# A projection in rounded parts: twelve more units per layer, contraction pieces outside, four units side by side in PSUM

## The reference

```
h = rms_norm(x, mix_norm[l])
p = h @ w_in[l]                # 1024 x 3200; in layer 1 also h @ vres_w_in (16 columns)
p_rwkv, p_conv, p_attn = p[..., :1280], p[..., 1280:2048], p[..., 2048:]
x = x + concat([rwkv7(p_rwkv), short_conv(p_conv), dilated_attention(p_attn)]) @ w_o[l]
x = x + ffn(rms_norm(x))       # layer 0: dense SwiGLU; layer 1: top 2 of 8 experts
```

## Time and profile before

| | us |
|---|---|
| median of three timed runs | 1656.16 |
| profiled execution, all of it | 1657.62 |
| its span | 1655.8 |
| TensorE busy in the span | 1605.9 |
| VectorE busy | 1213.1 |
| ScalarE busy | 1032.0 |
| projection of layer 0, first product to chunk 1's first | 21.05 to 93.05 |
| projection of layer 1, the same | 472.77 to 552.64 |

### The profile page before, as it was taken

The page is one execution under the profiler, slowest core; times in us unless marked ns, Lnnn a source line. Parts: engine busy times, 40 slices in busy tenths (PEclk is TensorE's granted clock), DMA queues, the critical chain, the costliest instruction groups (busy, mean ns, idle before and its releaser), DMA issues.

```text
span 1655.8 us, 28409 instructions
## 1 busy us (share of the span) xinstructions
PE 1605.9 (97%) x10904; PEld 1388.1 (84%) x10904; DVE 1213.1 (73%) x1378; ACT 1032.0 (62%) x1282; POOL 61.5 (4%) x70
## 2 busy tenths in 40 slices
PE   7998999999999999999999999999999999999997
PEld 6887889999988878888888888888888888888885
DVE  1465454545424664699999999999999999999996
ACT  2334344444423343488888888888887887888885
POOL 0003000000000040000000000000000100000000
PEclk8999999999989999899999999999999999999999
DMA  6502165555414301799999999999999999999994
GB/s 215 185 1 105 53 230 187 188 184 179 160 57 149 107 3 65 268 374 375 348 393 392 345 395 394 353 395 385 357 393 381 362 394 362 377 395 358 386 385 142
DMA packets 192503, 446.11 MB, mean 269 GB/s; under 512 B 9104, under 2 KB 11680, under 8 KB 192288
## 3 DMA queue, kind: packets, MB, share of 16 engines
q1 hardware_dynamic: 187040, 433.49, 71.4%
q0 software_dynamic: 2160, 7.87, 2.0%
q10 hardware_dynamic: 3216, 3.53, 0.6%
HBM read 438.56 MB, written 6.29 MB: 269 GB/s over the span
## 4 chain that ended last, share of the span: by engine, by line
PE 95%; DVE 2%; issue 1%; ACT 1%; DMA 0%; POOL 0%; SPq 0%; DVEq 0%; ACTq 0%; POOLq 0%
PE bank L700 24%; PE bank L702 24%; PE bank L701 24%; PE bank L683 15%; PE bank L796 3%; PE bank L1248 1%; PE bank L708 1%; DMA arena<-in_consts 0%; PE bank L1045 0%; ACT acts_hi L1312 0%; DVE acts_lo L2110 0%; PE bank L803 0%; DVE w_lo L1853 0%; DVE ring L1708 0%; PE bank L692 0%
## 5 line engine op out<-in xcount | busy, mean ns | idle before, releaser
L1312 ACT ACTIVATE w_hi<-ring 128x1024 fp32r<-128x1024 f32 x772 | 815.5, 1061 | 292.7 <-PE bank L702 292.0
L1862 DVE TENSOR_TENSOR w_lo<-ring,w_hi 128x1024 fp32r<-128x1024 f32 x672 | 812.9, 1224 | 64.1 <-ACT w_hi L1312 16.5
L700 PE MATMUL bank<-w_hi,acts_hi 128*128 128x512 f32 x1344 | 528.3, 393 | 7.1 <-DVE acts_lo L2110 5.7
L702 PE MATMUL bank<-w_hi,acts_lo 128*128 128x512 f32 x1344 | 523.7, 390 | 0.0
L701 PE MATMUL bank<-w_lo,acts_hi 128*128 128x512 f32 x1344 | 523.5, 389 | 0.0
L700 PEld LDWEIGHTS bank<-w_hi,acts_hi 128*128 128x128 f32 x1344 | 252.4, 188 | 59.8 <-issue 5.9
L702 PEld LDWEIGHTS bank<-w_hi,acts_lo 128*128 128x128 f32 x1344 | 252.3, 188 | 52.9
L701 PEld LDWEIGHTS bank<-w_lo,acts_hi 128*128 128x128 f32 x1344 | 252.5, 188 | 50.9
L1853 DVE TENSOR_TENSOR w_lo<-ring,w_hi 128x1024 fp32r<-128x1024 f32 x84 | 102.7, 1225 | 118.4 <-ACT w_hi L1312 118.4
L700 PE MATMUL bank<-acts_hi,w_hi 128*128 128x256 f32 x608 | 174.2, 286 | 1.6 <-DVE acts_lo L1671 1.6
L701 PE MATMUL bank<-acts_lo,w_hi 128*128 128x256 f32 x608 | 173.1, 285 | 0.0
(11 more groups left out here) (210 smaller groups left out, 1216.5 us busy)
## 6 DMA issues: line engine op xcount, KB each, us to landing
ring<-in_moe_wg SPq DMA_DIRECT2D x112, 1024.0 KB, 6.9
ring<-in_moe_wu SPq DMA_DIRECT2D x112, 1024.0 KB, 7.2
ring<-in_moe_wd SPq DMA_DIRECT2D x112, 1024.0 KB, 6.9
ring<-in_w_in SPq DMA_DIRECT2D x24, 1024.0 KB, 6.7
ring<-in_dense_wg SPq DMA_DIRECT2D x14, 1024.0 KB, 5.1
ring<-in_dense_wu SPq DMA_DIRECT2D x14, 1024.0 KB, 5.1
ring<-in_dense_wd SPq DMA_DIRECT2D x14, 1024.0 KB, 4.8
ring<-in_w_o SPq DMA_DIRECT2D x8, 1024.0 KB, 7.4
```

The source lines that it names most:

```text
L700: pe.matmul(out_, a_hi, b_hi, start=first, stop=False, **kw)
L702: return pe.matmul(out_, a_lo, b_hi, start=False, stop=final, **kw)
L1312: return act.activation(o, i, ACT.Copy, **kw)
L1862: TT(w_lo[:, q, :], raw, w_hi[:, q, :].bitcast(F32), ALU.subtract).then_inc(lo_ready, 1)
```

## The change

`SPLIT_IN` becomes (4, 5, 2, 0, 1): chunks 4, 5 and 0 are split too. Chunks 4, 5, 2 and 0 run through a new function, `project_together`: the four pieces of the contraction are the outer loop, and inside it the chunk's units take turns, two of them side by side in one bank. Each piece ends with an increment of `pc_free`, and ScalarE waits for it before it writes the piece of the next chunk. Chunk 1 is split, and runs unit by unit as before; chunks 6 and 3 stay in float32. Banks come from a table in place of g % 4. ScalarE copies a finished pair of units at once. Ring slots of split chunks are freed by VectorE's low parts. The head spread and the rotation now stand behind the second and fourth piece of chunk 2, the low-rank products w, a and g, v behind the second and fourth piece of chunk 0, and the head sum behind chunk 6. The low parts of the activations follow each scaling in all norms. For layer 1, three pieces of chunk 4 are split while the last dense product runs.

```
-        SPLIT_IN = (2, 1)
+        SPLIT_IN = (4, 5, 2, 0, 1)
+        TOGETHER = (4, 5, 2, 0)
+        UNIT_BANKS = {4: (0, 0, 1, 1), 5: (2, 2, 3, 3), 6: (0, 1, 0), 2: (2, 2, 3, 3), 0: (0, 0, 1, 1), 1: (2, 3, 0, 1),
+                      3: (2, 3, 0, 1)}
...
+                if ch in SPLIT_IN:
+                    stream += [("in", l, ch, hf, (lo_ready, IN0[l, ch] + 2 * hf + 2)) for hf in range(2)]
...
+            def project_together(l, ch, mine, us0, hooks):
+                for q in range(PIECES):
+                    pe.wait_ge(lo_ready, IN0[l, ch] + q + 1)
+                    if q == 0:
+                        seen = max(bank_place(l, us0 + i)[2] for i in range(len(mine)))
+                        if seen:
+                            pe.wait_ge(unit_kept, UNIT0[l] + seen)
+                    for i in range(2):
+                        k = 2 * q + i
+                        if ch == CHUNKS[0]:
+                            pe.wait_ge(h_low, KT * 2 * l + k + 1)
+                        for m, (kind, n) in enumerate(mine):
+                            b, at, _ = bank_place(l, us0 + m)
+                            o = bank[b][:, at:at + T]
+                            first, final = k == 0 and m % 2 == 0, k == KT - 1
+                            if kind == "cm":
+                                ws = slice(i * CW + n % 4 * P, i * CW + (n % 4 + 1) * P)
+                                last = three(o, w_hi[:, q, ws], w_lo[:, q, ws], h_hi[:, k, :], h_lo[:, k, :],
+                                             first, final, skip_group_check=True)
+                            else:
...
+                    last.then_inc(pc_free, 1)
+                    if q in hooks:
+                        hooks[q]()
...
+                HOOKS = {2: {1: lambda: head_spread(2 * l, 6, (5, 6, 7)), 3: turn_heads}, 0: {1: lora_wa, 3: lora_gv}}
...
@@ act: norm(n, ready, between, then_keep)
+                if n == 2:
+                    between(range(0, 3))
...
+                if n == 0:
+                    between(range(0, 2))
+                if n == 2:
+                    between(range(3, 4))
...
                 act.activation(rms, bank[SUM_BANKS[n]][:, 0:2], ACT.Sqrt, bias=eps, scale=1.0 / D).then_inc(rt_ready, 1)
+                if n == 0:
+                    between(range(2, 4))
...
@@ act: layer loop, behind high_h(2 * l)
+                split_in(l, 5, range(0, 3))
+                keep_pair(l, 4, "cm", 16)
+                keep_pair(l, 4, "cm", 18)
+                split_in(l, 5, range(3, 4))
+                split_in(l, 2, range(0, 3))
+                keep_pair(l, 5, "cm", 20)
+                act.wait_ge(unit_kept, kept(l, "cm", 21))
+                act.wait_ge(mask_set, 1)
+                act.activation(sq_qk, pT[:, 16:22, :], ACT.Square).then_inc(qk_sq, 1)
+                keep_pair(l, 5, "va", 0)
+                split_in(l, 2, range(3, 4))
+                for n in range(2):
+                    keep_unit(l, "vb", n)
+                if l:
+                    keep_unit(l, "vres", 0)
+                root(2 * l)
+                split_in(l, 0, range(0, 3))
+                keep_pair(l, 2, "cm", 8)
+                keep_pair(l, 2, "cm", 10)
...
+                split_in(l, 0, range(3, 4))
+                split_in(l, 1, range(0, 1))
...
+                split_in(l, 1, range(1, 4))
+                keep_pair(l, 0, "cm", 0)
+                keep_pair(l, 0, "cm", 2)
...
@@ dve: layer loop, behind norm(2 * l)
+                split_in(l, 5)
+                split_in(l, 2, range(0, 3))
                 head_factor(2 * l, 4, 1.0 / HD, NORM_EPS, (ALU.mult, ALU.add))
+                split_in(l, 2, range(3, 4))
+                split_in(l, 0, range(0, 1))
...
+                split_in(l, 0, range(1, 3))
                 dve.wait_ge(unit_kept, kept(l, "cm", 9))
...
+                split_in(l, 0, range(3, 4))
                 split_in(l, 1)
```

More of the change, by code:

```diff
@@ L472, in decoder_trunk, with singles, bank_place @@
         MOE0 = 2 * DENSE0 + 4 * 3 * NJ
+        def singles(l):
+            return [u for u in units(l) if CHUNKS[u[0]] not in TOGETHER]
+        def bank_place(l, u):
+            place = units(l)[u][0]
+            i = u - min(v for v, w in enumerate(units(l)) if w[0] == place)
+            b = UNIT_BANKS[CHUNKS[place]][i]
+            together = CHUNKS[place] in TOGETHER
+            at = i % 2 * T if together else 0
+            users = [v for v in range(u) if units(l)[v][0] != place or not together]
+            before_ = [v for v in users if UNIT_BANKS[CHUNKS[units(l)[v][0]]][
+                v - min(w for w, x in enumerate(units(l)) if x[0] == units(l)[v][0])] == b]
+            return b, at, (max(before_) + 1 if before_ else 0)
         def kept(l, kind, n):
@@ L1090, in _ @@
                     project(l, *unit, u)
[L1091 to L1093 removed]
+                    if ch == 6 and unit[4]:
                         pe.wait_ge(qk_sq, l + 1)
                         head_sum(2 * l, [sq_qk[:, i, :] for i in range(6)], 4)
[L1096 to L1102 removed]
@@ L1327, in high_h, with split_in @@
                     copy(h_hi[:, k, :], hT[:, k, :]).then_inc(h_high, 1)
-            def split_in(l, ch):
-                for q in range(4):
+            def split_in(l, ch, pieces=range(4)):
+                for q in pieces:
                     n = halves[("in", l, ch, q // 2)]
@@ L1373, in keep_unit, with keep_pair @@
                 ins.then_inc(unit_kept, 1)
+            def keep_pair(l, ch, kind, n):
+                act.wait_ge(pc_free, PIECES + IN0[l, ch] + PIECES)
+                b = bank[bank_place(l, [v[1:3] for v in units(l)].index((kind, n)))[0]][:, :]
+                b = b.rearrange("p (n t) -> p n t", n=2)
+                copy(pT[:, n:n + 2, :] if kind == "cm" else v_att[:, 0:2, 0:2 * P], b).then_inc(unit_kept, 2)
             def keep_lora(l, n, o, banks, func, bias):
@@ L1899, in _ @@
                     dve.wait_ge(vres_shifted, l)
+                dve.wait_ge(rot_done, l + 1)
+                for i in range(3):
+                    TT(sq_qk[:, 2 * i:2 * i + 2, :], bank[5 + i][:, :].rearrange("p (i t) -> p i t", i=2),
+                       spread(const("sin"), 2), ALU.mult)
+                qk = pT[:, 16:22, :]
+                then(TT(qk, qk, spread(const("cos"), 6), ALU.mult))
+                TT(qk, qk, sq_qk, ALU.add).then_inc(rope_ready, 1)
+                split_in(l, 0, range(3, 4))
                 split_in(l, 1)
```

168 lines of the change are left out of this document (78 added, 90 removed).

## The result

The changed kernel takes 1645.47 us (median of 5 timed runs, 1644.83 to 1647.86) where the kernel before takes 1656.16 us on the same chip (5 runs, 1653.33 to 1658.73): 10.7 us less, a ratio of 0.9934, 95% interval 0.9919 to 0.9950. The forecast was 1644.8 us with a range of 1639 to 1651. Its profiled execution was the slowest of its five, 1647.86 us with a span of 1646.1, so in the profiles the span is 9.7 us shorter than the 1655.8 before; 11.3 were forecast. It is the measure for all experiments; these ran on three chips, where the kernel before took 1658.7 to 1659.1 us.

What follows compares the result with a forecast made beforehand. TensorE's own work, 95% of the chain, bounds the kernel. Layer 0 gains 5.4 us, layer 1 5.5, the clock 0.4: 11.3 off 1657.6 gives 1646.3, less 1.5 for the timed median, 1644.8 us; range 1639 to 1651.

Steps and rivals of the forecast that it cites:

- Price of a unit: Projection: each unit of eight products gains 0.58 us in rounded parts instead of fp32; 24 units, 13.9 us.
- Splits and ring slots: Projection: added copies and subtractions hidden inside chunks 4, 5, 2 and 0; earlier ring loads worth nothing, cost nothing.
- Start of a layer: First product of each layer 0.9 us later, 0.3 more in layer 0; chunk 4 still gains 2.0 and 2.1 us.
- Waits at the ends of chunks: Three places losing cover: vres in layer 1 0.8 us, rope in layer 1 0.4, chunk 1 in layer 0 1.2.
- The clock: Layer 1's projection: two falls to half clock again, each costing 1.5 us in place of 1.7; 0.4 us gained.
- The recurrence: Behind the projection: keeps its order and shifts as a whole, with no gain or loss of its own.
- Two numbers of the last part: Signs to look for: chunk 1 of layer 1 at 546 to 547 us; chunk 4 ending near 35.5 and 486.5.
- The slower rival: Splits become serial at every chunk's start, 2.6 us at each of ten starts, 26 us: 1668.5 us; chance 0.04.

Runs made afterwards that it cites:

- both waits shortened: Changed kernel, with chunk 4's products with the activations' low part last and chunk 1 waiting for its low parts piece by piece: 1646.90 us, ratio 0.9932.

## Why the prediction was right, step by step

- **Price of a unit.** Right. 13.9 us forecast; 14.2 came back with the three chunks in fp32, 3.9 of 4.6 with chunk 0, and in the traces, without the falls of the clock, 7.0 of 6.96 and 2.05 of 2.3. Rounded matmuls stand 0.12 us apart as before, though each loads its own weights. The 20 us by the 109 ns of the Trainium skill (TensorE: Matmul & The Clock Gate, "Back-to-back issue gap") would have been too much; the page calls this the gap of an isolated matmul, which the prediction left out.
- **Splits and ring slots are worth nothing and cost nothing.** Right for both: one wait of 0.9 us on any of 40 subtractions, and no loss to be seen with the slots freed late. But it holds only because the pieces are the outer loop and because chunk 4 is split ahead of the norm. Exchanging the loops costs 48 us, the late split 14. The diff has two schedules that carry the gain without being any part of it, and the prediction passed over both in a sentence each ("three other pieces stand in between", "split under the last dense product").
- **Start of a layer.** The 0.9 us in layer 1 were 0.8. In layer 0, 2.8 us were lost where 1.2 were forecast, and my reason for 0.3 of these, a copy ahead of the table load, is not what made the difference: the kernels with slots freed late and with the subtraction doubled have the same copy there and start at 21.8 and 22.0 us, 0.8 and 1.0 later than the kernel before. In the changed kernel's profile the 32 sums of squares ran longer (7.0 us in place of 5). Among the kernels with the same instructions up to there, those that start at 21.7 to 22.0 us all had a stretch of 3.4 us of full clock from 12.1 to 12.6 us on, under the first sums; those that start at 23.5 to 23.9 had none. The Trainium skill (TensorE: Matmul & The Clock Gate, Part 1) has the chip watch activity free-running; the trace agrees, in that the same instructions fell both ways.
- **Waits at the ends of chunks.** All in the right places, all smaller than forecast: vres 0.29 (0.8), rope 0.29 (0.4), chunk 1 0.92 (1.2) in layer 0 and none in layer 1. The first is mis-sized by ScalarE's pair copies, 0.55 to 0.60 us and not twice 0.38: 0.4 us of the 0.5.
- **The clock.** This is the term that was wrong, twice, with opposite signs. Within layer 1's projection I took two falls again and got one, at 516.2 for 3.4 us: 1.5 us of the 2.8 by which that stretch beat its forecast. The smaller waits are 0.6 more. A further 0.5 us, in layer 0 too, is idle time ahead of the first low-rank product that the rows showed ("[0.49 <-issue]") and that is gone; the prediction did not count it. In the recurrence and ahead of the dense stage I took no difference and lost 3.0 us.
- **The recurrence.** The prediction put it at nothing, as a chain that shifts as a whole. It did not name the 3.7 us in which TensorE stands still there, and this is not the clock alone. The kernel with chunk 1 waiting piece by piece and the one with both waits shortened have the clock at half for 3.4 us in the recurrence, just as the kernel before; yet 500 products in they are 20.0 and 20.1 us behind its start, the kernel before 18.7, and TensorE is idle for 8.3 and 8.4 us in the recurrence, not 6.3. By the place of the stop: at 236 products in (the kernel before, three chunks in fp32) 500 products take 18.7 and 17.8 us; at 140 or some 172 in (the ten others), 20.0 to 21.5. Over the twelve profiles the whole stretch to layer 1's norm takes 337.2 and 338.4 us in those two and 339.7 to 341.4 in the ten. The longer half clock in some of them comes on top. What decides whether a fall behind the stop lasts 3.4 or 10.2 us is open.
- **Two numbers of the last part.** 546 to 547 us for chunk 1 of layer 1 left out layer 0's own gain; with it the forecast said 541.3, and 542.39 was measured. Chunk 4 ended at 37.5 in layer 0 (35.5 forecast, the late start) and 485.2 in layer 1 (486.5).
- **The slower rival** had its mechanism right, not its chance to occur: with splits exposed at chunk starts the time goes to 1660 to 1695. Its price of 26 us left out what follows a wait. In the exchanged loops 28 us of waits made 48.

## To carry to other kernels

Turning each fp32 product into three rounded ones was worth the difference of their issue intervals (0.58 us for eight products of 256 columns) as long as the splits were ahead; look at the order of loops first, since a buffer that is freed a piece at a time is what makes them cheap. A wait of TensorE ahead of a run of matmuls is to be priced above its length, because the clock can fall in it and stay down afterwards: 28 us of waits cost 48 here and 3.4 us cost 8, while the one wait of 0.92 us cost 1.0. After a wait in one engine's queue, look for what stands behind it: the 3 us ahead of the rotation were a wait for a scaling that stood in VectorE's queue behind a split. And count a row "issue" of some microseconds as a thing that can move when the number of instructions ahead of it changes.

## What the runs showed of the hardware

- The granted clock falls within waits and is low when the work resumes: 2.72 us of waiting, then chunk 1 at 14.1 us in place of 11.5; 5.73 us, then 0.50 over the next four microseconds. A wait is not a place where half clock passes at no cost: with 8.2 us of waiting at a layer's start, the first products were still at half.
- Layer 0's first product, behind the same instructions, stands at 21.7 to 22.0 us in some kernels and at 23.5 to 23.9 in others. These 2 us are half clock under the sums of squares, and here they were carried on: with a start 2.1 us earlier, the kernel with late slots had its chunk 1 of layer 1 at 539.86, 2.5 us earlier.
- In the recurrence TensorE stands still for 1.5 to 4.1 us behind its 856th matmul record (two profiles: 855th) in all twelve profiles, with nothing shown that it waits for, and goes on 2.4 to 2.65 us behind the start of a 16 KB packet on the instruction queue; eleven of the twelve stop again, for 1.2 to 3.9 us, behind the 983rd.
- A copy of 512 columns from PSUM takes ScalarE 0.55 to 0.60 us, one of 256 columns 0.38: pairs save about a quarter.
